# Norm boundaries: the last two squares summed on TensorE, products of high parts first, three first FFN tiles, and fillers in TensorE's pauses

## The chip, the cores and the metric

The kernel runs on one core of a Trainium2 chip. The metric is the device time of one execution in microseconds, taken as the median of several runs of the whole program. A profiled execution gives the trace that all rows below come from.

## What is computed

One step of a four-layer transformer backbone on 128 context tokens and 512 latent tokens (640 columns with margins: 644), model width 1024. Each layer is a token mixer followed by a gated ConvFFN, and each of the eight sub-layers starts with the same normalisation:

```python
def rmsnorm(x, g):
    y = x * rsqrt(mean(x * x, axis=-1) + EPS)
    return y * g
def modulate(h, shift, scale):
    return h * (1 + scale) + shift
...
for i in range(4):                     # mixers: pooling, GQA, differential, windowed GQA
    h = modulate(rmsnorm(x, norm1_g[i]), sh1, sc1)
    x = x + g1 * mixer_i(h)
    h = modulate(rmsnorm(x, norm2_g[i]), sh2, sc2)
    u = conv3(h @ w_in)                # 1024 -> 2 x 2816, three taps along the tokens
    a, b = split(u)
    x = x + g2 * ((silu(a) * b) @ w_out)
```

`sh`, `sc` and `g` come from a matrix product of the conditioning vectors with `w_mod` (1024 x 6144 for each layer). All arithmetic is float32.

## The kernel before

The state `x` lies transposed in SBUF as `xT`: eight slices (index d or k) of 128 channels by 644 columns. Every float32 product of the projections is made of three reduced-precision products: activations and weights are split into a high part (`h_hi`, `w_hi`) and a remainder (`h_lo`, `w_lo`), and `hi*hi`, `lo*hi` and `hi*lo` are summed in PSUM. `product` (L1941) issues these three for one output.

The order of the work is written out by hand, engine by engine; semaphores connect the engines. PSUM is two tensors of four banks: `psA` and `psB`.

**A norm boundary** is the place between the last product of one sub-layer and the first of the next. There are seven of them with the same code, n = 1 to 7 (the first norm of layer 0 has its own). Even n is the way from an FFN into the QKV products of layers 1, 2 and 3; odd n is the way from a mixer into the FFN. On the path lie:

- ScalarE squares each slice (`square`, L2165): slice 0 into `sq_sum`, slices 1 to 7 by turns into `sq[0]` and `sq[1]`.
- GpSimd adds slices 1 to 6 to `sq_sum` (`norm_pow`, L1892), VectorE adds slice 7 (L2337).
- TensorE sums over the 128 channels with the squares as stationary operand and a 128x2 tile of ones as the moving one (`norm_pe`, L1999; L2007), one product for each of five token tiles, into `psB`. The program's records show two matmuls for each, as for every plain float32 product here.
- VectorE turns the sums into means (`ms`, L2351), GpSimd takes the power -1/2 (`rs`, L1900), TensorE transposes and broadcasts it (L2017) to `psB`.
- VectorE scales each slice (`xs`, L2368), ScalarE adds the shift and rounds (`h_hi`, L2191), VectorE takes the remainder (`h_lo`, L2378). Two slices are in work at a time.

At n = 2 to 6 TensorE also runs a piece of the next modulation there (`mod_gap`, 64 short products of L1961 into `psA`, ahead of the sums, and its four transposes L1969 ahead of those of `rs`). At n = 1 it is `mod_raw(10)`, whose weights come by DMA.

**Even n, after the norm:** `qkv_step` (L2040). For each slice k, four output tiles (i = 0 to 3, token tiles, 512 columns each, one bank of `psA` each) get their three products; then i = 4 and on, tile by tile. ScalarE squares and copies tile i when its last product is done (L2225, L2226), VectorE and GpSimd norm and rotate it (L1463 and on), and VectorE's `w_lo` for the next weights (L2290) is queued behind the third of them.

**Odd n, after the norm:** `first_u_tiles` (L2090). Two FFN tiles (ft = 0, 1) of 128 channels by 644 columns (two halves of 322) are made together, slice by slice; then tile 2 and tile 3, each alone. ScalarE evacuates tile ft (`evac`, L2240), then makes two units of `w_hi` for the next weights (`split_next`), then evacuates tile ft + 1. Tile 2 uses the banks of tile 0, and tile 3 those of tile 1:

```python
def u_tile(it, ft, first):
    if not (first and ft < 2):
        pe.wait_ge(s_u[l], it * 4 + (ft - 1))
```

An FFN has 11 such rounds, and TensorE has no pause in one of them that matters here. `load_w`, `load_wo` and `load_m` are SyncE's DMA issues.

## Time and profile before

| | |
|---|---|
| median of 3 runs | 3270.67 us (3270.58 to 3274.07) |
| profiled execution, its own time | 3271.68 us |
| its span, first to last instruction | 3269.8 us |
| mean granted TensorE clock | 0.967 |
| TensorE matmul busy | 3083.9 us, 94% |
| VectorE, ScalarE, GpSimd busy | 2107.2, 1071.4, 403.9 us |
| the seven `ms` instructions (L2351) start at | 86.9, 617.0, 959.8, 1481.3, 1921.7, 2443.7 and 2776.7 us |

A row of the timeline gives start, duration, engine, line, operation and tiles; the bracket is the idle time of that engine before it and the instruction that ended it. Several instructions of one kind in a row are merged (x10). The granted clock is 1.00 at 2.4 GHz and 0.50 at 1.2 GHz.

### The profile page before, as it was taken

The page shows a single profiled execution, that of the slowest core. Times are in us where ns is not written, and L with a number is a line of the kernel's source. Part 1 is how long each engine was busy: PE and PEld are TensorE (multiplying, and loading weights), DVE is VectorE, ACT ScalarE, POOL GpSimd, SP SyncE. Part 2 cuts the span into 40 slices and gives each one's busy share as a digit, 9 for nine tenths or more (in the row PEclk, how much of TensorE's full clock was granted, in tenths as well). Part 3 has the DMA queues.
Part 4 walks back from the last instruction along what each step waited for, and adds up shares of the span by engine and source line. Part 5 has one row for each costly group of instructions (what it writes and reads, how often), then busy time and mean ns, then how long its engine had stood idle before and what let it go on. Part 6 is the DMA issues. An engine that isn't in the chain of part 4 may idle for free.

```text
span 3269.8 us, 54337 instructions
## 1 busy us (share of the span) xinstructions
PE 3083.9 (94%) x21098; PEld 2813.1 (86%) x21098; DVE 2107.2 (64%) x4290; ACT 1071.4 (33%) x2074; POOL 403.9 (12%) x392
## 2 busy tenths in 40 slices
PE   8999999888999999998989899999989888999998
PEld 6899999766599999997865699999987668999998
DVE  7666666567756666656646566666666674766665
ACT  3222222326623222223335432222223563322221
POOL 3000000123310000003237310000012231000000
PEclk9999999889999999999988999999999899999999
DMA  8533323110023332330200223333321002122211
GB/s 336 198 116 128 115 97 113 54 55 1 22 95 129 120 124 91 114 116 31 78 30 6 93 78 116 112 120 117 127 73 52 4 1 91 65 78 77 67 62 45
DMA packets 47188, 289.96 MB, mean 89 GB/s; under 512 B 4945, under 2 KB 11345, under 8 KB 13265
## 3 DMA queue, kind: packets, MB, share of 16 engines
q1 hardware_dynamic: 47058, 288.21, 24.2%
q8 instruction: 83, 1.36, 0.2%
q14 instruction: 47, 0.39, 0.0%
HBM read 283.98 MB, written 4.21 MB: 88 GB/s over the span
## 4 chain that ended last, share of the span: by engine, by line
PE 89%; DVE 6%; ACT 2%; issue 1%; DMA 1%; POOL 0%; SPq 0%; POOLq 0%; DVEq 0%; ACTq 0%
PE psA L1945 39%; PE psB L1945 25%; PE psA L2046 3%; PE psA L2048 3%; PE psA L2047 3%; PE psB L1961 2%; PE psA L779 2%; PE psB L712 2%; PE psB L694 1%; PE psB L837 1%; PE psA L680 1%; DVE top L1671 1%; DVE top L1558 1%; DVE query L1514 1%; DMA m_stage<-w_mod_dram 1%
## 5 line engine op out<-in xcount | busy, mean ns | idle before, releaser
L1945 PE MATMUL psA<-h_hi,w_hi 128*128 128x322 f32 (+1 forms) x2848 | 661.2, 314 | 13.7 <-DVE h_lo L2378 13.7
L1945 PE MATMUL psA<-h_lo,w_hi 128*128 128x322 f32 (+1 forms) x2832 | 657.7, 313 | 0.0
L1945 PE MATMUL psA<-h_hi,w_lo 128*128 128x322 f32 x2816 | 648.4, 311 | 0.0
L2405 DVE SCALAR_TENSOR_TENSOR xT<-psB,mod,xT 128x128 f32<-128x128 f32 x1128 | 425.4, 433 | 249.8 <-PE psB L1945 249.8
L1945 PEld LDWEIGHTS psA<-h_hi,w_hi 128*128 128x128 f32 x2848 | 481.3, 190 | 17.1 <-issue 15.7
L1945 PEld LDWEIGHTS psA<-h_lo,w_hi 128*128 128x128 f32 x2832 | 482.7, 190 | 0.0
L1945 PEld LDWEIGHTS psA<-h_hi,w_lo 128*128 128x128 f32 x2816 | 480.1, 190 | 0.0
L2459 DVE TENSOR_SCALAR conv<-u_raw,vec_sb 128x642 f32<-128x642 f32 x176 | 108.3, 615 | 468.6 <-ACT u_raw L2244 468.6
L2244 ACT ACTIVATE u_raw<-psA 128x644 f32<-128x644 f32 x176 | 124.6, 708 | 741.2 <-PE psA L1945 741.2
L2290 DVE TENSOR_TENSOR w_lo<-w_stage,w_hi 128x512 fp32r<-128x512 f32 x496 | 345.9, 743 | 27.1 <-ACT w_hi L2163 27.0
L1945 PE MATMUL psB<-g_hi,wo_hi 128*128 128x322 f32 x1408 | 335.6, 320 | 23.7 <-DVE g_lo L2480 23.7
L1945 PE MATMUL psB<-g_hi,wo_lo 128*128 128x322 f32 x1408 | 326.7, 314 | 0.0
L1945 PE MATMUL psB<-g_lo,wo_hi 128*128 128x322 f32 x1408 | 326.6, 313 | 0.0
L1898 POOL TENSOR_TENSOR sq_sum<-sq_sum,sq 128x644 f32<-128x644 f32 x42 | 71.3, 1698 | 1721.4 <-ACT sq L2180 1720.8
L1945 PEld LDWEIGHTS psB<-g_hi,wo_hi 128*128 128x128 f32 x1408 | 237.6, 192 | 38.2 <-DVE g_lo L2480 24.8
L2274 ACT ACTIVATE wo_hi<-wo_stage 128x1024 fp32r<-128x1024 f32 x88 | 88.4, 1053 | 554.5 <-PE psB L1945 554.5
L1945 PEld LDWEIGHTS psB<-g_lo,wo_hi 128*128 128x128 f32 x1408 | 241.2, 192 | 0.0
L1945 PEld LDWEIGHTS psB<-g_hi,wo_lo 128*128 128x128 f32 x1408 | 241.1, 191 | 0.0
L2046 PE MATMUL psA<-w_hi,h_lo 128*128 128x512 f32 x480 | 195.6, 408 | 26.0 <-DVE w_lo L2290 16.2
L2250 ACT ACTIVATE w_hi<-w_stage 128x512 fp32r<-128x512 f32 x344 | 196.7, 624 | 0.0
L2047 PE MATMUL psA<-w_hi,h_hi 128*128 128x512 f32 x480 | 193.4, 403 | 0.0
L2048 PE MATMUL psA<-w_lo,h_hi 128*128 128x512 f32 x480 | 193.2, 403 | 0.0
(257 smaller groups left out, 4526.3 us busy)
## 6 DMA issues: line engine op xcount, KB each, us to landing
w_stage<-weights_dram SPq DMA_DIRECT2D x124, 1024.0 KB, 4.9
m_stage<-w_mod_dram SPq DMA_DIRECT2D x96, 1024.0 KB, 8.3
wo_stage<-w_out_dram SPq DMA_DIRECT2D x44, 1024.0 KB, 4.8
yT_dram<-xT SPq DMA_DIRECT2D x8, 322.0 KB, 2.2
xT<-xT_dram SPq DMA_DIRECT2D x1, 1544.0 KB, 9.9
xT<-xT_dram SPq DMA_DIRECT2D x1, 1032.0 KB, 6.4
w_stage<-weights_dram SPq DMA_DIRECT2D x2, 512.0 KB, 17.8
rope_raw<-rope_dram SPq DMA_DIRECT2D x3, 256.0 KB, 2.7
```

The costliest lines, as they stand in the source:

```text
L712: ins = pe.matmul(OUT_LAT[odd * DH:(odd + 1) * DH, x:y], value(kt, 2 * d // GROUP), pt[(2 * d + odd) % 4][:, kt - 1, x:y], start=(kt == CA ...
L1898: pool.tensor_tensor(sq_sum[:, :], sq_sum[:, :], sq[d % 2][:, :], ALU.add).then_inc(s_sqsum, 1)
L1945: ins = pe.matmul(o, wp, xp[:, a:b], start=first and n == 0, stop=last and n == 2)
L2046: pe.matmul(o, hl, w_hi[:, k, :], start=(k == 0), stop=False)
L2047: pe.matmul(o, hh, w_hi[:, k, :], start=False, stop=False)
L2048: return pe.matmul(o, hh, w_lo[:, k, :], start=False, stop=(k == KT - 1))
L2244: act.activation(u_raw[ft % 2][:, :].rearrange("p (a n) -> p a n", a=2), psA[:, 2 * (ft % 2):2 * (ft % 2) + 2, 0:HALF], ACT.Copy).then_inc ...
L2250: act.activation(w_hi[:, u, :], w_stage[:, u, :], ACT.Copy).then_inc(s_whi, 1)
L2274: act.activation(wo_hi[:, f, :], wo_stage[:, f, :], ACT.Copy).then_inc(s_wohi, 1)
L2290: dve.tensor_tensor(w_lo[:, u, :], w_stage[:, u, :], w_hi[:, u, :].bitcast(F32), ALU.subtract).then_inc(s_wlo, 1)
L2405: ins = dve.scalar_tensor_tensor(out=xT[:, d, c:c + w], in0=psB[:, bank, at_:at_ + w], scalar=gate[:, d, i:i + 1], in1=xT[:, d, c:c + w], ...
L2459: own(dve.tensor_scalar(o[:, 1:1 + n], u[:, 1:1 + n], vcol(v + 1), vcol(v + 3), ALU.mult, ALU.add))
```

## The change

- **Sums.** VectorE's addition of slice 7 (L2337) goes, and GpSimd's of slice 6. TensorE now sums three tiles, `sq_sum` (slices 0 to 5), `sq[0]` (slice 6) and `sq[1]` (slice 7), each with five products, accumulated in `psA`, bank 0. Ahead of them one product with a tile of zeros (`zeros`, ten columns) clears the ten sums.
- **Fillers.** `keep_on(count, out)` runs `count` float32 products of the identity with a 128x128 tile of ones into a bank that nobody reads. Ten at n = 7 ahead of the sums; three ahead of the wait for `rs` (n = 2 to 7), six behind the transposes of `rs` (n = 2 to 7).
- **Order of products.** In the first group after each norm, the two products with `h_hi` of all tiles come first and wait for `h_hi` alone; those with `h_lo` follow. For i = 4 and on the order inside a step changes only.
- **Three tiles.** At n = 3, 5 and 7 tiles 0, 1 and 2 are made together; tile 2 goes to banks 0 and 1 of `psB`. At n = 1 it stays at two.

```diff
             def norm_pow(n):
                 m = n - 1
-                for d in range(1, KT - 1):
+                for d in range(1, KT - 2):
...
             def norm_pe(n, gap=None):
                 if gap is not None:
                     mod_gap(*gap)
+                elif n == 2 * DEPTH - 1:
+                    keep_on(10, psA[:, 0, :])
                 if n == 1:
                     pe.wait_ge(s_modok, MOD_PASSES - 2)
-                pe.wait_ge(s_sqall, n)
-                for j in range(NT):
-                    c = tile_col(j)
-                    ins = pe.matmul(psB[:, 0, 2 * j:2 * j + 2], sq_sum[:, c:c + P], ones2[:, :],
-                                    start=True, stop=True)
+                pe.matmul(psA[:, 0, 0:2 * NT], ident[:, :], zeros[:, :], start=True, stop=False, skip_group_check=True)
+                for i, x in enumerate((sq_sum, sq[0], sq[1])):
+                    if i == 0:
+                        pe.wait_ge(s_sqsum, (KT - 3) * n)
+                    pe.wait_ge(s_sq, KT * n - 2 + i)
+                    for j in range(NT):
+                        c = tile_col(j)
+                        ins = pe.matmul(psA[:, 0, 2 * j:2 * j + 2], x[:, c:c + P], ones2[:, :],
+                                        start=False, stop=(i == 2), skip_group_check=True)
                 ins.then_inc(s_stat, 1)
                 if gap is not None:
                     mod_gap_sum(*gap)
                 if n == 1:
                     mod_raw(10)
+                else:
+                    keep_on(3, psB[:, 1, :])
                 pe.wait_ge(s_rs, n)
...
                 ins.then_inc(s_bc, 1)
+                if n > 1:
+                    keep_on(6, psB[:, 1, :])
...
                     for k in range(KT):
                         pe.wait_ge(s_wlo, UNITS * c0 + k + 1)
+                        pe.wait_ge(s_hhi, KT * (2 * l - 1) + k + 1)
+                        for i in range(4):
+                            qkv_hi(i, k)
                         pe.wait_ge(s_h, KT * (2 * l - 1) + k + 1)
                         for i in range(4):
-                            ins = qkv_step(i, k)
+                            ins = qkv_lo(i, k)
                             if k == KT - 1:
                                 ins.then_inc(s_qp[l], 1)
...
+                    places = [halves(psA, 0), halves(psA, 1), halves(psB, 0)][:2 if l == 0 else 3]
...
-                dve.wait_ge(s_sqsum, (KT - 2) * n)
-                dve.wait_ge(s_sq, KT * n)
-                dve.tensor_tensor(sq_sum[:, :], sq_sum[:, :], sq[(KT - 1) % 2][:, :], ALU.add).then_inc(s_sqall, 1)
```

TensorE at the boundary n = 2, from the end of the modulation's products (L1961) to the first QKV products, before (`ones_139` is the 128x2 tile of ones):

```order
L1961 MATMUL psA<-m_stage_58,cond 32x128 x32
L2007 MATMUL psB<-ones_139,sq_sum 128x2 x5
L1969 MATMUL psA<-ident_sb,mod_rows 128x128 x4
L2017 MATMUL psB<-ident_sb,rs 128x128 x5
L2046 MATMUL psA<-w_hi,h_lo 128x512
L2047 MATMUL psA<-w_hi,h_hi 128x512
L2048 MATMUL psA<-w_lo,h_hi 128x512
```

and in the change:

```order
L1961 MATMUL psA<-m_stage_58,cond 32x128 x32
L2013 MATMUL psA<-zeros,ident_sb 128x10
L2020 MATMUL psA<-ones_139,sq_sum 128x2 x5
L2020 MATMUL psA<-ones_139,sq_67 128x2 x5
L2020 MATMUL psA<-ones_139,sq_68 128x2 x5
L1969 MATMUL psA<-ident_sb,mod_rows 128x128 x4
L2002 MATMUL psB<-ones,ident_sb 128x128 x3
L2032 MATMUL psB<-ident_sb,rs 128x128 x5
L2002 MATMUL psB<-ones,ident_sb 128x128 x6
L2063 MATMUL psA<-w_hi,h_hi 128x512
L2064 MATMUL psA<-w_lo,h_hi 128x512
```

Ten narrow products and one with the zeros came in ahead of the means, three fillers between the modulation's transposes and those of `rs`, and six ahead of the first product of the layer.

TensorE at n = 3, from the last transposes to the end of the first slice of the FFN's first tiles, in the change:

```order
L2032 MATMUL psB<-ident_sb,rs 128x128 x5
L2002 MATMUL psB<-ones,ident_sb 128x128 x6
L2133 MATMUL psA<-h_hi,w_hi 128x322 x2
L2133 MATMUL psA<-h_hi,w_lo 128x322 x2
L2133 MATMUL psA<-h_hi,w_hi 128x322 x2
L2133 MATMUL psA<-h_hi,w_lo 128x322 x2
L2133 MATMUL psB<-h_hi,w_hi 128x322 x2
L2133 MATMUL psB<-h_hi,w_lo 128x322 x2
L2138 MATMUL psA<-h_lo,w_hi 128x322 x4
L2138 MATMUL psB<-h_lo,w_hi 128x322 x2
```

Before, a slice was twelve products for two tiles, all behind `h_lo`; now it is eighteen for three, twelve of them ahead of `h_lo`, and the last products of tiles 0, 1 and 2 stand next to each other at the slice's end.

## Rows read from the trace of the kernel before

**Rows 1.** The page: the chain that ended last, share of the span by engine

```profile
PE 89%; DVE 6%; ACT 2%; issue 1%; DMA 1%; POOL 0%; SPq 0%; POOLq 0%; DVEq 0%; ACTq 0%
```

**Rows 2.** Timeline of the boundary n = 2 (start us, us, engine, line)

```profile
612.64 1.96 PE L1961 MATMUL psA<-m_stage,cond 128*32 128x128 f32 x64
...
614.76 0.83 DVE L2337 TENSOR_TENSOR sq_sum<-sq_sum,sq 128x644 f32<-128x644 f32 x1 [0.88 <-ACT sq L2180]
...
615.64 1.28 PE L2007 MATMUL psB<-ones,sq_sum 128*128 128x2 f32 x10 [1.05 <-DVE sq_sum L2337]
616.96 0.17 DVE L2351 TENSOR_SCALAR ms<-psB 128x5 f32<-128x5 f32 x1 [1.28 <-PE psB L2007]
...
618.44 1.33 PE L2017 MATMUL psB<-ident_sb,rs 128*128 128x128 f32 x5
...
623.05 0.77 PE L2046 MATMUL psA<-w_hi,h_lo 128*128 128x512 f32 x1 [3.29 <-DVE h_lo L2378]
```

**Rows 3.** Timeline of the boundary n = 3

```profile
954.53 1.38 ACT L2180 ACTIVATE sq<-xT 128x644 f32<-128x644 f32 x2
955.05 2.63 DVE L2290 TENSOR_TENSOR w_lo<-w_stage,w_hi 128x512 fp32r<-128x512 f32 x2
...
958.51 1.28 PE L2007 MATMUL psB<-ones,sq_sum 128*128 128x2 f32 x10 [2.67 <-DVE sq_sum L2337]
959.83 0.16 DVE L2351 TENSOR_SCALAR ms<-psB 128x5 f32<-128x5 f32 x1 [1.28 <-PE psB L2007]
...
963.97 1.93 ACT L2191 ACTIVATE h_hi<-xs,mod 128x128 fp32r<-128x128 f32 x4 [8.07 <-DVE xs L2368]
...
966.18 0.88 PE L1945 MATMUL psA<-h_hi,w_hi 128*128 128x322 f32 x2 [3.29 <-DVE h_lo L2378]
```

**Rows 4.** TensorE by stretches: length, busy (records), granted clock, DMA share, GB/s

```profile
623.00:628.30 5.30, 5.25 (x12) 0.50 0.00 0
956.00:959.50 3.50, 0.99 (x9) 1.00 0.26 47
966.10:969.60 3.50, 3.42 (x13) 0.50 0.00 0
970.00:973.00 3.00, 3.00 (x23) 1.00 0.00 0
...
93.00:99.40 6.40, 6.00 (x22) 0.50 1.00 419
```

**Rows 5.** Timeline of TensorE at n = 7

```profile
2774.33 2.30 PE L2007 MATMUL psB<-ones,sq_sum 128*128 128x2 f32 x10 [4.55 <-DVE sq_sum L2337]
...
2782.76 0.88 PE L1945 MATMUL psA<-h_hi,w_hi 128*128 128x322 f32 x2 [3.29 <-DVE h_lo L2378]
```

**Rows 6.** Timeline at the end of the first QKV group of layer 1

```profile
645.66 0.39 PE L2048 MATMUL psA<-w_lo,h_hi 128*128 128x512 f32 x1
...
646.09 0.60 ACT L2225 ACTIVATE qkv_sq<-psA 128x512 f32<-128x512 f32 x1 [11.26 <-PE psA L2048]
...
659.12 0.77 PE L2046 MATMUL psA<-w_hi,h_lo 128*128 128x512 f32 x1 [5.39 <-DVE w_lo L2290]
```

**Rows 7.** Timeline of ScalarE and TensorE after the FFN's first two tiles (n = 3)

```profile
981.52 0.71 ACT L2244 ACTIVATE u_raw<-psA 128x644 f32<-128x644 f32 x1 [3.55 <-PE psA L1945]
...
982.28 0.56 PE L1945 MATMUL psA<-h_hi,w_hi 128*128 128x322 f32 x2
...
983.17 0.70 ACT L2244 ACTIVATE u_raw<-psA 128x644 f32<-128x644 f32 x1
```

**Rows 8.** The chain in order of time: float32 products of 136 or 144 columns

```profile
20.90 2.10 PE psB L1064 x16
...
32.74 2.23 PE psA L1064 x8
```

**Rows 9.** Timeline of TensorE at n = 1

```profile
89.35 0.76 PE L2017 MATMUL psB<-ident_sb,rs 128*128 128x128 f32 x5
...
93.40 0.88 PE L1945 MATMUL psA<-h_hi,w_hi 128*128 128x322 f32 x2 [2.51 <-DVE h_lo L2378]
```

More of the change, by code:

```diff
@@ L232, in program @@
         ones = const("ones", [P, P])
+        zeros = const("zeros", [P, 2 * NT])
         sq_tok = const("sq_tok", [P, NT])
@@ L296, in program @@
         s_rs = sem("norm_rstd_ready")
-        s_sqall = sem("all_squares_added")
         s_bc = sem("rstd_broadcast")
@@ L1997, in mod_gap_sum, with keep_on @@
                 mod_sum(it * 2 + (MOD_PASSES * (2 * l + 1) + 2), [psA[:, c, 3 * P:] for c in range(4)])
+            def keep_on(count, out):
+                for _ in range(count):
+                    pe.matmul(out[:, 0:P], ident[:, :], ones[:, :], start=True, stop=True)
             def norm_pe(n, gap=None):
@@ L2040, in _, with qkv_hi, qkv_lo @@
                 else:
-                    def qkv_step(i, k):
+                    def qkv_hi(i, k):
                         o, col = psA[:, i % 4, :], tile_col(i % NT)
-                        hh, hl = h_hi[:, k, col:col + P], h_lo[:, k, col:col + P]
-                        pe.matmul(o, hl, w_hi[:, k, :], start=(k == 0), stop=False)
-                        pe.matmul(o, hh, w_hi[:, k, :], start=False, stop=False)
-                        return pe.matmul(o, hh, w_lo[:, k, :], start=False, stop=(k == KT - 1))
+                        hh = h_hi[:, k, col:col + P]
+                        pe.matmul(o, hh, w_hi[:, k, :], start=(k == 0), stop=False)
+                        pe.matmul(o, hh, w_lo[:, k, :], start=False, stop=False)
+                    def qkv_lo(i, k):
+                        o, col = psA[:, i % 4, :], tile_col(i % NT)
+                        return pe.matmul(o, h_lo[:, k, col:col + P], w_hi[:, k, :], start=False, stop=(k == KT - 1))
                     for k in range(KT):
                         pe.wait_ge(s_wlo, UNITS * c0 + k + 1)
+                        pe.wait_ge(s_hhi, KT * (2 * l - 1) + k + 1)
+                        for i in range(4):
+                            qkv_hi(i, k)
                         pe.wait_ge(s_h, KT * (2 * l - 1) + k + 1)
                         for i in range(4):
-                            ins = qkv_step(i, k)
+                            ins = qkv_lo(i, k)
                             if k == KT - 1:
@@ L2100, in first_u_tiles @@
                             mod_raw_sum(11)
+                        pe.wait_ge(s_hhi, KT * 2 * l + k + 1)
+                        for ft, outs in enumerate(places):
+                            u, c = 2 * ft + k // 4, (k % 4) * P
+                            for n, w in enumerate((w_hi, w_lo)):
+                                for o, (a, b) in outs:
+                                    pe.matmul(o, w[:, u, c:c + P], h_hi[:, k, a:b], start=(k == 0 and n == 0), stop=False)
                         pe.wait_ge(s_h, KT * 2 * l + k + 1)
-                        for ft in range(2):
+                        for ft, outs in enumerate(places):
                             u, c = 2 * ft + k // 4, (k % 4) * P
-                            ins = product(halves(psA, ft), (w_hi[:, u, c:c + P], w_lo[:, u, c:c + P]),
-                                          (h_hi[:, k, :], h_lo[:, k, :]), k == 0, k == KT - 1)
-                            if ft == 0 and k in (3, 7):
-                                ins.then_inc(s_wused, 1)
-                    ins.then_inc(s_wused, 2)
+                            for o, (a, b) in outs:
+                                ins = pe.matmul(o, w_hi[:, u, c:c + P], h_lo[:, k, a:b], start=False, stop=(k == KT - 1))
+                            if k == 3 and ft == 0 or k == 7:
+                                ins.then_inc(s_wused, 2 if ft else 1)
                 def out_pass(it, last=False):
@@ L2138, in ffn_iter @@
                         mod_ffn(l, 0, 1)
-                    u_tile(it, 2, first)
+                    if not first or l == 0:
+                        u_tile(it, 2, first)
                     if not first and l < DEPTH - 1:
@@ L2243, in evac @@
                         act.wait_ge(s_conv[l], it * 4 + (ft - 1))
-                    act.activation(u_raw[ft % 2][:, :].rearrange("p (a n) -> p a n", a=2),
-                                   psA[:, 2 * (ft % 2):2 * (ft % 2) + 2, 0:HALF], ACT.Copy).then_inc(s_u[l], 1)
+                    src = psB[:, 0:2, :] if first and l and ft == 2 else psA[:, 2 * (ft % 2):2 * (ft % 2) + 2, :]
+                    act.activation(u_raw[ft % 2][:, :].rearrange("p (a n) -> p a n", a=2), src[:, :, 0:HALF],
+                                   ACT.Copy).then_inc(s_u[l], 1)
                 def split_next(it, ft):
@@ L2413, in _ @@
             own(dve.memset(ones2[:, :], 1.0))
+            own(dve.memset(zeros[:, :], 0.0))
             own(dve.memset(ones[:, :], 1.0))
```

11 lines of the change are left out of this document (6 added, 5 removed).

## The prediction, as put on record before the changed kernel was run

> **What bounds the kernel now.** I read the chain that ended last first: TensorE holds 89% of it, VectorE 6% [rows 1]. So time is won where TensorE pauses or runs at half clock, and lost where it gets more to do or waits longer. Then the timeline of the boundaries, for who ends each pause. At n = 2 TensorE is done with the modulation at 614.60 (612.64 + 1.96), VectorE's addition starts at 614.76, the ten narrow records take 1.28 us, the means come at 616.96, and the first QKV product starts at 623.05 [rows 2]. At n = 3 the squares are there at 955.91, but VectorE is busy with two `w_lo` for 2.63 us, and TensorE sums only at 958.51; means at 959.83, first product at 966.18, while the first slice of `h_hi` is done half of 1.93 us after 963.97, at 964.94 [rows 3]. Last the granted clock by stretches: it is 1.00 while TensorE does little but the narrow products (0.99 us busy in 3.5), then 0.50 into the first products: 5.3 us of products at n = 2 and 3.5 at n = 3 [rows 4].
>
> **The sum, forecast case: the clock falls as before.** All lengths are against before; M is the start of the means.
>
> 1. *Sums.* 30 narrow records and 2 for the zeros replace 10. At 1.28/10, less the tail of the last, one costs 0.12 us [rows 2], so 32 take 3.9. At even n they run from 614.60, to 618.5, and M is 1.6 us later: before, TensorE had only waited 1.05 us there. At n = 3 and 5 they run from 955.85 to 959.75 against M at 959.83: nothing. VectorE's addition, its `w_lo` slowed by GpSimd (1.3 us each) and the wait for them were in the way before; TensorE's own work takes exactly their place. At n = 7 there is no modulation; ten fillers (term 2) last 2.6 us, then 3.9, from about 2769.8: M at 2776.3 against 2774.33 + 2.30 = 2776.63: -0.3. At half clock a narrow record costs 0.23 [rows 5]; the fall can come in the midst of them. Bounds 0 and +1.5 us at each place, taken as +0.4, since most positions of the fall lie near their end.
> 2. *Three fillers.* One is two records. Float32 products of 136 to 144 columns go at 0.131 us a record at full clock and 0.279 at half [rows 8]; I take 0.13 and, for 128 columns, 0.26. Three cost 0.8 or 1.6 us. At n = 2 to 6 they stand between the modulation's transposes, which wait for two copies by VectorE, and those of `rs`. The latter started 1.48 us after M at n = 2 [rows 2], with `rs` just ready, so there is no pause to fill: the cost is whole, 0.75 at full clock, 1.6 at half. At n = 7 the wait for `rs` (1.4 us) covers them: 0.
> 3. *High parts first.* The first product waits for `h_hi` and no longer for `h_lo`: 966.18 - 964.98 = 1.2 us earlier [rows 3]. But six fillers stand ahead of it, 1.6 us at full clock and 3.1 at half, beside 2.05 us for the first `xs` and `h_hi`. At half clock they end last by 0.95; the fillers are long enough that the clock may be back before they end, so I take 0.3. Net -0.9, at n = 7 -0.2 (nothing else delays the fillers there).
> 4. *Cold products.* TensorE now works without a pause from M + 0.9 to its first product, longer than the 3.5 to 5.3 us of products after which the clock came back before [rows 4], so the first products run at full clock. Saved: half of the cold stretch. At 0.233 against 0.426 us a QKV product, 5.3 us lose 2.4 [rows 4]; n = 4 and 6, read the same way, lost 2.0 and 2.1. At 0.149 against 0.267 an FFN product, 3.5 us lose 1.56 [rows 4]; n = 5 lost 1.9 and n = 7 1.35.
> 5. *QKV group, even n.* A chain of ScalarE, VectorE and GpSimd starts when tile i = 0 has its last product, 646.09, and releases TensorE 13 us later, after a pause of 5.39 us [rows 6]. In the last slice tile 0's third product had nine behind it; now it has three. With 0.233 us each, the chain starts 1.4 us later against the group's end, and nothing covers it. +1.4.
> 6. *Three tiles, n = 3, 5, 7.* Tile 3 needs the banks of tile 1. ScalarE evacuates tile 0, makes two `w_hi`, evacuates tile 1: from 981.52 to 983.17 + 0.70, 2.35 us. Tile 2 covered that; TensorE went on at 982.28 [rows 7]. Now tile 0's last product is five records before the group's end, and TensorE waits for both: 2.35 less about 0.4: +1.9. What three tiles give is that TensorE cannot run dry for `h`: a slice is 2.7 us of products, against 1.96 us for VectorE's work on it. Before it was 1.8, but started late and cold and never ran dry, so there is nothing to win unless the clock holds.
>
> Even n: 1.6 + 0.4 + 1.6 - 0.9 - 2.2 + 1.4 = +1.9, with the cold transposes of n = 2 (full clock before) +2.1; three of them 6. n = 3 and 5: 0.4 + 1.6 - 0.9 - 1.7 + 1.9 = +1.3 each, 2.6. n = 7: 0.1 - 0.2 - 1.35 + 1.9 = +0.4. n = 1: 22 records more, 2.6 us, ahead of `mod_raw(10)` and the transposes, less 1.2 for `h_hi`; before, TensorE was idle 2.51 us ahead of 93.40 [rows 9] and then half as fast for 6.4 us [rows 4], and a later start may keep the clock. Bounds -1.8 and +1.1: I take 0. Removing GpSimd's addition and VectorE's costs and gives nothing more. Sum **+9 us** on the profiled execution's 3271.68, or 3280.7; the median lies 1.0 under that execution: **3280**.
>
> **Why the clock should fall.** Between the modulation's products and its transposes TensorE now has only products of two columns for nearly 4 us, and then the copies' pause of 0.9. In the trace of before ten of them, and what little stood beside them, never held it: 956.0 to 959.5 is such a stretch, and half clock follows [rows 4]. The fillers stand behind, not in it; the ten at n = 7 stand ahead. The Trainium skill, "TensorE: Matmul & The Clock Gate", section "Why this matters for your kernels", asks only that there be no long gaps in which TensorE idles between bursts. By that rule the narrow products would keep it and the first rival holds; the rows lean the other way.
>
> **Rival 1, the clock holds (0.25): faster.** Its place is the stretch of sums, and it decides at the point where narrow products count as work. Then term 1's 0.4 goes, term 2 is 0.75, the transposes of `rs` take 0.76 us as at n = 1 [rows 9] and not 1.3 (-0.55), the six fillers are covered, and the cold products are saved whole. Even n: 1.6 + 0.75 - 0.55 - 1.2 - 2.2 + 1.4 = -0.2 to -0.3; n = 3 and 5: 0.75 - 0.55 - 1.2 - 1.75 + 1.9 = about -1; n = 7: -1.5; n = 1: -1.8. Sum -6.6: 3264, between 3261 and 3269. For it: the fillers are there in all the other pauses. Against it: rows 4.
>
> **Rival 2, the fillers do not bring it back (0.1): slower still.** Then the change does not do what it says: term 4 returns (11 us in all) and six fillers at half clock cost 0.65 more at five places. 3280 + 11 + 3 = 3294. The same skill page, section "Part 4: PE-mode transpose", says that transposes don't count as work for the clock; at full weight that speaks for this rival. But the fillers are plain products, and dense ones brought it back at every boundary before.
>
> **Rival 3, a cover (0.1): no change.** Term 5 or 6 is partly hidden by a wait that is there anyway, say VectorE's or GpSimd's; 1 us less at each of six places gives 3274. Against it: rows 6 and 7 show the wait ended by just those chains.
>
> **The numbers.** Forecast 0.55, its own range 3275 to 3287; rival 1 0.25, rival 2 0.1, rival 3 0.1. The range that leaves out no more than 2 in 10 reaches into rival 1 and short of rival 2: 3262 to 3289. 0.2% is 6.5 us (about what can be told from no change): faster, under 3264.1, is half of rival 1 and its odd neighbours, 0.2; same, to 3277.2, is the rest of it, rival 3 and the forecast's lower end, 0.3; slower 0.5.
>
> **What would show it.** Right: half clock from within or just behind the thirty narrow records; means 1.6 us or more later after the modulation at even n and level at n = 3; the transposes of `rs` starting 2.2 us (full clock) or 3.4 (half) after M; first products at full clock; the pause of 5.4 us in QKV unchanged or longer, and counted from tile 0; a new pause of about 2 us of TensorE before tile 3, ended by ScalarE's `u_raw`, at three places. Wrong: a clock of 1.00 through a whole boundary, narrow records faster than 0.12 us, or no pause before tile 3.

## The result, and the profile after

The changed kernel takes 3285.87 us (median of 6, 3275.59 to 3289.9) against 3274.1 us for the kernel before (median of 6, 3270.58 to 3277.71): 1.003 of its time, 95% interval 1.0018 to 1.0042, so slower by 11.8 us. The profiled execution of the changed kernel is the fastest of its six. A second series of both, among the experiments, gave 3283.7 against 3271.3 us, a ratio of 1.0037 (1.0024 to 1.0051); the profile taken there (run e1_same, span 3283.8 us, itself 3285.54 us) is of an ordinary execution, so rows of both are read.

Page of the changed kernel, the lines that answer to [rows 1] and to the table of before:

```profile
span 3273.8 us, 54877 instructions
...
PE 89%; DVE 6%; ACT 2%; issue 1%; DMA 1%; POOL 0%; SPq 0%; POOLq 0%; DVEq 0%; ACTq 0%
...
L1945 PE MATMUL psA<-h_hi,w_hi 128*128 128x322 f32 (+1 forms) x2672 | 617.6, 312 | 5.5 <-ACT u_raw L2278 5.5
```

TensorE keeps its 89% of the chain. In the page of before the row of these products has 13.7 us of pauses, ended by `h_lo`; new are 5.5 us of pauses ended by ScalarE's `u_raw`, which are the three pauses ahead of tile 3.

Timeline of the changed kernel at n = 2, against [rows 2] (L2020 sums, L2002 fillers, L2032 transposes of `rs`, L2063 first QKV product):

```profile
610.66 1.95 PE L1961 MATMUL psA<-m_stage,cond 128*32 128x128 f32 x64
...
612.79 1.26 PE L2020 MATMUL psA<-ones,sq_sum 128*128 128x2 f32 x10
613.91 2.37 PE L2020 MATMUL psA<-ones,sq 128*128 128x2 f32 x20
616.32 0.17 DVE L2381 TENSOR_SCALAR ms<-psA 128x5 f32<-128x5 f32 x1 [4.33 <-PE psA L2020]
...
619.39 0.97 PE L2032 MATMUL psB<-ident_sb,rs 128*128 128x128 f32 x5
620.20 1.50 PE L2002 MATMUL psB<-ones,ident_sb 128*128 128x128 f32 x12
...
622.60 0.47 PE L2063 MATMUL psA<-w_hi,h_hi 128*128 128x512 f32 x1 [0.90 <-ACT h_hi L2224]
```

From the start of the modulation's products to the means it was 4.32 us and is 5.66: 1.34 later, since the thirty records stand one behind the other and nothing fills in for them. From the means to the transposes of `rs` it was 1.48 and is 3.07: the three fillers. The first product comes 6.28 us behind the means where it came 6.09 behind; the wait is ended by `h_hi` now. And it starts at full clock. TensorE by stretches, the first three answering to the first three in [rows 4], the last one behind tile 3's start (stretch, length, busy with records, granted clock, DMA share, GB/s):

```profile
622.60:626.00 3.40, 3.40 (x15) 1.00 0.00 0
956.00:959.50 3.50, 2.57 (x19) 0.76 0.68 267
966.00:969.50 3.50, 3.50 (x26) 1.00 0.00 0
988.70:991.90 3.20, 3.20 (x13) 0.50 0.00 0
```

So in this profile the clock fell within or behind the sums at every boundary and was back by the first products or within the first few, as forecast. The last row was not forecast. Ahead of it stands the pause before tile 3, here in the timeline of n = 3, against [rows 7]:

```profile
985.58 0.71 ACT L2278 ACTIVATE u_raw<-psA 128x644 f32<-128x644 f32 x1 [8.44 <-PE psA L2138]
...
986.18 1.14 ACT L2284 ACTIVATE w_hi<-w_stage 128x512 fp32r<-128x512 f32 x2
...
987.22 0.70 ACT L2278 ACTIVATE u_raw<-psA 128x644 f32<-128x644 f32 x1
...
987.97 0.56 PE L1945 MATMUL psA<-h_hi,w_hi 128*128 128x322 f32 x2 [1.84 <-ACT u_raw L2278]
```

ScalarE's two evacuations with two `w_hi` between them are bare now: 1.84 us of pause, and then 3.2 us of products at 1.2 GHz. And this is the end of the first QKV group of layer 1, against [rows 6]:

```profile
644.46 0.60 ACT L2258 ACTIVATE qkv_sq<-psA 128x512 f32<-128x512 f32 x1 [9.03 <-PE psA L2069]
...
645.60 0.49 PE L2063 MATMUL psA<-w_hi,h_hi 128*128 128x512 f32 x1 [0.47 <-ACT qkv L2259]
...
657.49 0.77 PE L2063 MATMUL psA<-w_hi,h_hi 128*128 128x512 f32 x1 [6.06 <-DVE w_lo L2324]
```

The pauses there add up to 6.53 us where there was one of 5.39, and the same two stand at the other two even boundaries.

The split sums cost most at n = 1. Timeline of the changed kernel, and then the same rows of e1_same:

```profile
84.58 1.26 PE L2020 MATMUL psA<-ones,sq_sum 128*128 128x2 f32 x10
85.70 2.82 PE L2020 MATMUL psA<-ones,sq 128*128 128x2 f32 x20
...
88.56 0.16 DVE L2381 TENSOR_SCALAR ms<-psA 128x5 f32<-128x5 f32 x1 [4.07 <-PE psA L2020]
```

```profile
84.69 2.27 PE L2020 MATMUL psA<-ones,sq_sum 128*128 128x2 f32 x10
86.83 4.41 PE L2020 MATMUL psA<-ones,sq 128*128 128x2 f32 x20
...
91.27 0.16 DVE L2381 TENSOR_SCALAR ms<-psA 128x5 f32<-128x5 f32 x1 [6.87 <-PE psA L2020]
```

And the kernel before:

```profile
86.89 0.16 DVE L2351 TENSOR_SCALAR ms<-psB 128x5 f32<-128x5 f32 x1 [1.16 <-PE psB L2007]
```

The squares are long there, but the sums stand behind TensorE's wait for the modulation. So all thirty are on the path, and the means wait 4.07 us for them where the clock falls only near their end and 6.87 where it has fallen ahead of them, in place of 1.16.

### The profile page after: what moved, and what is told of

Same layout as the page of the kernel before. It is cut to its first block, busy times and chain, and to the rows that moved or that the text cites. A ratio compares the mean times of both kernels' runs of the same rounds, so it can differ in the third digit from the quotient of the medians.

```text
span 3273.8 us, 54877 instructions
## 1 busy us (share of the span) xinstructions
PE 3112.8 (95%) x21380; PEld 2843.2 (87%) x21380; DVE 2097.1 (64%) x4284; ACT 1071.3 (33%) x2074; POOL 392.1 (12%) x385
## 4 chain that ended last, share of the span: by engine, by line
PE 89%; DVE 6%; ACT 2%; issue 1%; DMA 1%; POOL 0%; SPq 0%; POOLq 0%; DVEq 0%; ACTq 0%
PE psA L1945 36%; PE psB L1945 25%; PE psA L2063 3%; PE psA L2064 3%; PE psA L2069 3%; PE psB L1961 2%; PE psA L779 2%; PE psB L712 2%; PE psA L2133 1%; PE psB L694 1%; PE psB L837 1%; PE psA L680 1%; PE psA L2020 1%; DVE top L1671 1%; PE psA L2138 1%
## 5 line engine op out<-in xcount | busy, mean ns | idle before, releaser
L1945 PE MATMUL psA<-h_hi,w_hi 128*128 128x322 f32 (+1 forms) x2672 | 617.6, 312 | 5.5 <-ACT u_raw L2278 5.5
L1945 PE MATMUL psA<-h_lo,w_hi 128*128 128x322 f32 (+1 forms) x2656 | 615.0, 312 | 0.0
L1945 PE MATMUL psA<-h_hi,w_lo 128*128 128x322 f32 x2640 | 606.8, 311 | 0.0
L1945 PEld LDWEIGHTS psA<-h_hi,w_hi 128*128 128x128 f32 x2672 | 450.1, 190 | 6.9 <-ACT u_raw L2278 6.3
L1945 PEld LDWEIGHTS psA<-h_lo,w_hi 128*128 128x128 f32 x2656 | 450.9, 189 | 0.0
L1945 PEld LDWEIGHTS psA<-h_hi,w_lo 128*128 128x128 f32 x2640 | 448.6, 190 | 0.0
L1898 POOL TENSOR_TENSOR sq_sum<-sq_sum,sq 128x644 f32<-128x644 f32 x35 | 59.5, 1699 | 1704.7 <-ACT sq L2213 1704.3
L2063 PE MATMUL psA<-w_hi,h_hi 128*128 128x512 f32 x480 | 192.5, 401 | 21.3 <-DVE w_lo L2324 18.2
L2069 PE MATMUL psA<-w_hi,h_lo 128*128 128x512 f32 x480 | 179.0, 397 | 0.0
```

The lines of the kernel that those rows point to most:

```text
L1945: ins = pe.matmul(o, wp, xp[:, a:b], start=first and n == 0, stop=last and n == 2)
L2063: pe.matmul(o, hh, w_hi[:, k, :], start=(k == 0), stop=False)
L2069: return pe.matmul(o, h_lo[:, k, col:col + P], w_hi[:, k, :], start=False, stop=(k == KT - 1))
```

## The experiments

Each was timed in 5 rounds beside the kernel before on the same chip; the medians of before in the four series, on three chips, are 3271.3, 3271.0, 3271.18 and 3270.63 us.

**How to tell the boundaries from the rest.** Two executions of one kernel can lie several us apart, and not at the boundaries: inside the attention of layers 1 to 3 TensorE falls to half clock in other places from profile to profile. So I divide each profiled execution at marks that every version has:

- *to n = 2*: from the start to the modulation's products at n = 2, with the boundary n = 1 in it;
- *sums*: at n = 2 to 6 from the modulation's first product to the means, at n = 7 from the end of the last product of the mixer to the means, six in all;
- *behind, even*: from the means of n = 2, 4 and 6 to TensorE's first product behind the pause for `w_lo` [rows 6];
- *behind, odd*: from the means of n = 3, 5 and 7 to the start of ScalarE's sixth `u_raw`;
- *attention*: what lies between the marks of an even boundary and the next odd one.

The rest, the FFNs of layers 1 to 3, is 1374.0 to 1375.9 us in all of them. Lengths in us, worked out from the timelines; each is of one execution:

| profiled execution | to n = 2 | sums | behind, even | behind, odd | attention |
|---|---|---|---|---|---|
| before | 612.6 | 31.7 | 126.0 | 153.8 | 971.4 |
| the change | 610.7 | 35.1 | 124.3 | 157.2 | 971.8 |
| e1_same | 611.4 | 35.9 | 124.5 | 156.5 | 981.0 |
| e2_two_tiles | 609.9 | 36.5 | 124.4 | 152.0 | 973.9 |
| e3_qkv_last_slice | 611.0 | 35.1 | 120.1 | 155.0 | 978.3 |
| e4_no_fillers | 613.1 | 32.3 | 127.2 | 161.8 | 972.3 |
| e5_both_repairs | 612.2 | 34.6 | 120.3 | 152.8 | 975.4 |
| e6_old_sums | 607.4 | 30.7 | 119.9 | 152.7 | 972.7 |
| e7_wide_sums | 615.2 | 36.2 | 115.5 | 149.1 | 971.8 |
| e8_hi_first_alone | 607.9 | 31.7 | 123.8 | 154.0 | 975.6 |
| e9_old_sums_wide | 604.9 | 31.0 | 118.6 | 152.8 | 973.0 |
| e10_no_fillers | 607.1 | 32.1 | 123.3 | 153.9 | 976.0 |
| e11_old_sums_n1 | 608.0 | 35.2 | 120.5 | 152.6 | 977.1 |
| e12_rstd_first | 606.3 | 30.7 | 120.1 | 152.6 | 973.2 |

The attention column spreads over 9.6 us, more than most of the effects below. That it goes with the clock shows in its longest piece, layer 2 from n = 4 to n = 5. Two stretches there, both from 14 us behind the means of n = 4 to 7 us ahead of those of n = 5, first in e9_old_sums_wide and then in e10_no_fillers:

```profile
1485.80:1902.32 416.52, 381.33 (x1828) 0.94 0.14 51
```

```profile
1488.26:1911.20 422.94, 388.36 (x1834) 0.92 0.14 50
```

Why a version shows one pattern or the other, no run tells.

**The change again.** No edit.

> The changed kernel once more, beside the three that follow. Theory A (the clock falls in the narrow sums, the fillers bring it back, and the three costs of the prediction stand): 0.2 to 0.4% above the kernel before, 3278 to 3288 us, half clock again behind the sums at each of the seven boundaries. Theory B (the loss is the place at which the clock happens to fall and differs from execution to execution): in this profile at least two boundaries keep full clock, and the median lies within 0.1% of the kernel before.

Measured: 3283.7 us (3282.93 to 3287.52), 1.0037 (1.0024 to 1.0051) of before. This is what the next three are held against. Half clock stands at all seven boundaries, so theory B fails in its own terms. For the size it has a point: against the profile of before, e1_same is 14.0 us longer, and 9.6 of these lie in the attention, where the clock falls in other places.

**Two first tiles.**

```
-                    places = [halves(psA, 0), halves(psA, 1), halves(psB, 0)][:2 if l == 0 else 3]
+                    places = [halves(psA, 0), halves(psA, 1), halves(psB, 0)][:2]
...
-                    if not first or l == 0:
-                        u_tile(it, 2, first)
+                    u_tile(it, 2, first)
```

> The FFN starts with two tiles at n = 3, 5 and 7, as before; all else as changed. Theory A: the pause of TensorE before tile 3 (about 2 us at three places) goes; TensorE may run dry for h now and then, up to 0.2 us a slice, so 3 to 5.5 us less than the changed kernel. Theory C (three tiles pay, because TensorE would starve with two at full clock): as slow or slower than the changed kernel, with pauses of TensorE that end with h_hi or h_lo of more than 2 us at each place.

Measured: 3274.9 us (3271.77 to 3280.39), 1.0011 (1.0001 to 1.002), 8.8 us below e1_same, more than either theory allowed. Page of this run, the row for ScalarE's pauses; then TensorE behind tile 3's start at n = 3, in e1_same:

```profile
L1945 PE MATMUL psA<-h_hi,w_hi 128*128 128x322 f32 (+1 forms) x2720 | 627.6, 312 | 1.5 <-ACT u_raw L2277 1.5
```

```profile
988.00:990.00 2.00, 0.56 (x4) 1.00 0.00 0
990.00:991.50 1.50, 1.10 (x7) 1.00 0.00 0
991.50:995.00 3.50, 3.50 (x15) 0.51 0.00 0
```

The pauses fall from 5.5 to 1.5 us. With the pause the fall of the clock behind it goes too: it stands in e1_same behind two of the three places (here, and behind tile 3 of the last FFN), in this run behind none. A fall of about 3.4 us at 1.2 GHz loses 1.7 us, so 4.0 + 3.4 = 7.4 us come back there. But something is paid for it: with two tiles at full clock TensorE does run dry for `h_lo`, as theory A allowed. Its products with `h_lo`, slice by slice at n = 3, start every 1.96 us, which is VectorE's pace, where twelve records take 1.8:

```profile
969.81 0.87 PE L2138 MATMUL psA<-h_lo,w_hi 128*128 128x322 f32 x4
...
971.77 0.88 PE L2138 MATMUL psA<-h_lo,w_hi 128*128 128x322 f32 x4
```

Net, the odd boundaries are 4.5 us shorter (156.5 to 152.0). The rest of the 8.8 us lies elsewhere: the attention is 7.1 us shorter in this profile.

**The last slice of the QKV group tile by tile.**

```
-                        for i in range(4):
-                            qkv_hi(i, k)
+                        if k < KT - 1:
+                            for i in range(4):
+                                qkv_hi(i, k)
                         pe.wait_ge(s_h, KT * (2 * l - 1) + k + 1)
                         for i in range(4):
+                            if k == KT - 1:
+                                qkv_hi(i, k)
                             ins = qkv_lo(i, k)
```

> In the first QKV group the last slice (k = 7) goes tile by tile again, the other seven with high parts first. Theory A: the chain that starts with tile 0's last product starts 1.4 us earlier at n = 2, 4 and 6: 4 us less than the changed kernel. Rival: VectorE or GpSimd is late there anyway, under 1 us.

Measured: 3275.59 us (3269.36 to 3278.66), 1.0008 (0.9999 to 1.0017), 8.1 us below e1_same. The wait is back at the 5.39 us of before:

```profile
656.55 0.77 PE L2063 MATMUL psA<-w_hi,h_hi 128*128 128x512 f32 x1 [5.39 <-DVE w_lo L2327]
```

It is so at all three even boundaries. By the waits that is 1.14 us at each; from the means to the end of the pause it is 1.57, 1.37 and 1.44, together 4.4 us (124.5 to 120.1), as theory A has it. The other 3.7 us are not the edit's as far as the traces show: 2.7 us of attention, and a fall of the clock behind one tile 3 less.

**Without fillers.** All calls of `keep_on` are out.

> No fillers at all. Theory A: three fillers ahead of the transposes cost 0.8 to 1.3 us at five places, but the clock comes back later, with 2 us lost at six places: 0 to 8 us more than the changed kernel. Rival (fillers only delay, the clock does not follow them): 4 to 8 us less than the changed kernel.

Measured: 3282.74 us (3279.46 to 3284.27), 1.0032 (1.002 to 1.0043): 1 us below e1_same, within what the two medians can tell. In its trace the clock stays down into the first products at n = 3 (0.88 us for the first pair, where it was 0.53), while the first product comes 5.29 us behind the means and not 6.30. The traces say why the median hardly moves. Behind the means this run is 8.0 us longer than e1_same (2.7 at even n, 5.2 at odd n), the sums are 3.6 shorter, half of that the ten fillers of n = 7, and the attention happens to be 8.7 shorter. So the fillers pay at the boundaries here as well, and the attention hides it.

**Both repairs together.** The edits of e2_two_tiles and of e3_qkv_last_slice.

> The change with both repairs together: only two first FFN tiles, and the last slice of the QKV chain tile by tile. Theory A (each of the two gives back its own wait and the half-clock stretch behind it, apart from the other): the 8.8 us of e2_two_tiles and the 8.1 us of e3_qkv_last_slice add up, 3283.7 - 16.9 = 3267, below the kernel before. Theory B (the waits proper are 5.5 us before tile 3 plus about 1.7 us of half clock behind each of one to three of them, and 1.1 us x 3 in the QKV group, and the rest of both results was which stretches of the attention fell to the half clock in those executions): 3283.7 - 9 to -12 = 3272 to 3275.

Measured: 3273.69 us (3271.96 to 3274.82), 1.0005 (0.9996 to 1.0014). Theory B: 10.0 us below e1_same, where the two single results add up to 16.9 and the waits and falls seen in the traces to 10.8. So what the single runs gave beyond that was not theirs. Behind the means the trace has 7.9 us for both (4.2 at even n, 3.7 at odd n), and the pauses are those of the single runs.

**The sums of before.** On e5_both_repairs.

```
-                for d in range(1, KT - 2):
+                for d in range(1, KT - 1):
...
+                dve.wait_ge(s_sqsum, (KT - 2) * n)
+                dve.wait_ge(s_sq, KT * n)
+                dve.tensor_tensor(sq_sum[:, :], sq_sum[:, :], sq[(KT - 1) % 2][:, :], ALU.add).then_inc(s_sqall, 1)
...
-                pe.matmul(psA[:, 0, 0:2 * NT], ident[:, :], zeros[:, :], start=True, stop=False, skip_group_check=True)
-                for i, x in enumerate((sq_sum, sq[0], sq[1])):
...
+                pe.wait_ge(s_sqall, n)
+                for j in range(NT):
+                    c = tile_col(j)
+                    ins = pe.matmul(psB[:, 0, 2 * j:2 * j + 2], sq_sum[:, c:c + P], ones2[:, :],
+                                    start=True, stop=True)
```

> e5_both_repairs with the sums of the kernel before: POOL adds squares 1 to 6, VectorE adds the last, and TensorE makes one set of five products. Theory A (the prediction's term for the split sums: 16 us x 0.1, that is 1.6 us later means at each of the three even boundaries, and an earlier fall of the clock at all of them): 4 to 8 us below e5. Rival (the split sums take as much out of the odd boundaries, or keep the engine busy where it would idle, as they cost at the even ones): within 2 us of e5, or above it.

Measured: 3260.2 us (3259.5 to 3262.12), 0.9964 (0.9951 to 0.9977): 13.5 us below e5_both_repairs and 10.8 below the kernel before. That is 5.5 more than I expected at most, so the split sums are the dearest part of the change. Its timeline at n = 2:

```profile
607.42 1.95 PE L1962 MATMUL psA<-m_stage,cond 128*32 128x128 f32 x64
...
610.42 1.28 PE L2017 MATMUL psB<-ones,sq_sum 128*128 128x2 f32 x10 [1.05 <-DVE sq_sum L2369]
...
614.75 1.27 PE L2029 MATMUL psB<-ident_sb,rs 128*128 128x128 f32 x5
...
618.26 0.47 PE L2060 MATMUL psA<-w_hi,h_hi 128*128 128x512 f32 x1 [0.78 <-ACT h_hi L2223]
```

The means are back at 4.32 us behind the modulation (611.74), and with the fillers the clock is back before the first product, which takes 0.47 us (0.77 at half clock, in [rows 2]).

**Wide sums.** On e5_both_repairs, with `ones[:, 0:64]` as the moving operand in place of the two columns of `ones2`, the sums 64 columns apart, and `zeros` as wide. TensorE's records are no longer for it: at full clock ten take 1.22 us where they took 1.26.

> e5_both_repairs with 64 columns in place of 2 in each product of the sums (the same sums in every column). Theory A (the half clock comes because products of two columns keep TensorE busy in the records but do not count for the clock): the fall in the sums goes or moves behind the wait for rs, less half clock at each boundary, and 3 to 10 us below e5. Rival (the waits around the sums drop the clock whatever the sums hold): the same places of the falls, within 2 us of e5.

Measured: 3267.21 us (3256.3 to 3268.88), 0.9982 (0.9973 to 0.9991), 6.5 us below e5_both_repairs. This is the stretch from 5 us ahead of the means to 13 us behind them, at n = 1, 2 and 3, in e5_both_repairs and then with wide sums:

```profile
85.85:103.85 18.00, 16.20 (x109) 0.74 0.73 309
613.11:631.11 18.00, 17.06 (x127) 0.81 0.09 30
953.52:971.52 18.00, 17.07 (x149) 0.81 0.18 59
```

```profile
87.83:105.83 18.00, 16.20 (x95) 0.64 0.64 266
616.17:634.17 18.00, 16.17 (x130) 1.00 0.10 30
956.23:974.23 18.00, 16.18 (x147) 1.00 0.18 59
```

At all six boundaries from n = 2 on the clock is 1.00 throughout, with the same waits, the same number of records issued and the same fillers. So from n = 2 on it was the narrow operand that let the clock fall. Behind the means that gives 8.6 us (120.3 to 115.5 and 152.8 to 149.1); the means themselves come up to 0.37 us later, since the product with `zeros` is 320 columns wide now. At n = 1 the clock fell before the sums began, and they cost more than ever. The Trainium skill, "TensorE: Matmul & The Clock Gate", section "Why this matters for your kernels", asks only for no long gaps between bursts; here the records alone, without a gap, did not hold the clock, so on this point the trace disagrees.

**High parts first, alone.** On the kernel before, the split into `qkv_hi` and `qkv_lo` and the same order for the two first FFN tiles, the last QKV slice tile by tile.

> The kernel before with one part of the change alone, the high parts ahead of the low parts (the last slice of the QKV chain tile by tile). By the prediction's term of 0.9 us at six boundaries: 5 us below the kernel before, 3266. Rival (the first products run at the half clock there, so that the start moves ahead but the chain is set by TensorE behind it, or the clock's return takes what was won): within 2 us of the kernel before.

Measured: 3269.36 us (3268.23 to 3271.7), 0.9992 (0.9983 to 1.0001): 1.6 us below before, its interval reaches 1. The first product does come 5.31 us behind the means at n = 2 in place of 6.09, and the wait is ended by `h_hi`, but it starts cold:

```profile
617.52 0.77 PE L2046 MATMUL psA<-w_hi,h_hi 128*128 128x512 f32 x1 [2.24 <-ACT h_hi L2207]
...
607.21:625.21 18.00, 13.78 (x113) 0.72 0.10 31
```

So the median says the rival. The trace says where it holds: at n = 3, 5 and 7 nothing is left at the sixth `u_raw` (154.0 against 153.8; e2_two_tiles shows VectorE's pace for `h` setting the length there); at the even boundaries 2.3 us are won, and 4.7 by n = 2, at n = 1, where the stretch at half clock is half as long as before. The attention was 4.1 us longer in this profile.

**The sums of before, wide.** On e6_old_sums, 64 columns in its five products.

> e6_old_sums with 64 columns in place of 2 in its five products a boundary. In e7 thirty wide ones held the clock at every boundary; in e6 ten records of two columns are still followed by 3.4 us at half clock at each of six boundaries. Theory A (columns, not records, hold the clock, and ten wide records do it as well): these six stretches go, 1.7 us each in the work done, up to 10 us: 3250 to 3256. Rival (with so few records it is the pause before and behind them that drops it): as e6, 3260, within 2 us.

Measured: 3261.84 us (3256.68 to 3267.39), 0.9973 (0.9964 to 0.9982). The rival: no gain over e6_old_sums (the medians differ by 1.6 us the other way). In the stretches around the means the clock is 1.00 at n = 1 and 2, 0.91 at n = 3 to 6 and 0.81 at n = 7. At n = 3 VectorE's addition leaves a pause of 2.67 us ahead of the sums, but at n = 4 and 6 the pause is that of n = 2 (1.0 us) and the clock falls all the same. So ten wide products did not hold it as thirty did; which of the pauses around them decides is not shown.

**The same without fillers.** On e9_old_sums_wide, no `keep_on`.

> e9_old_sums_wide without any of the fillers. Theory A (the change's fillers bring the clock back in the waits for rs and h_hi, which is what pays; in e4 they paid nothing because the thirty narrow records had used the place up): 5 to 10 us above e9. Rival (with wide sums there is enough dense work at a boundary without them, and they stand in the way of rs's transposes): within 2 us of e9 or below it.

Measured: 3268.11 us (3266.91 to 3271.41), 0.999 (0.9981 to 0.9999), 6.3 us above e9_old_sums_wide. The stretches around the means at n = 3 and 7, first of e9_old_sums_wide, then of this run:

```profile
944.89:962.89 18.00, 13.50 (x115) 0.91 0.18 59
...
2757.36:2775.36 18.00, 14.89 (x91) 0.81 0.18 58
```

```profile
947.71:965.71 18.00, 12.17 (x92) 0.72 0.18 58
...
2768.14:2786.14 18.00, 11.69 (x57) 0.62 0.17 58
```

0.72 and 0.62 are also what the kernel before has at these two places. So the fillers do what the change says. What they pay can be read behind the means: 4.7 us at the even boundaries and 1.0 at the odd ones, and 1.0 more in the sums of n = 7, 6.8 in all and near the difference of the medians. The two profiled executions lie 10.3 apart; the rest is mostly attention (3.1) and the stretch to n = 2 (2.1), which holds no filler. At n = 3 the fillers win nothing: the sixth `u_raw` starts 51.43 us behind the means with them and 51.45 without.

**The sums of before at n = 1 alone.** On e5_both_repairs.

```
+                if n == 1:
+                    pe.wait_ge(s_sqall, 1)
+                    for j in range(NT):
+                        c = tile_col(j)
+                        ins = pe.matmul(psB[:, 0, 2 * j:2 * j + 2], sq_sum[:, c:c + P], ones2[:, :],
+                                        start=True, stop=True)
+                else:
```

> e5_both_repairs with the sums of the kernel before at n = 1 alone (POOL adds six squares there, VectorE the last, one set of five products); the split sums stay at the other six boundaries. In the traces the thirty records stand there wholly in the path, behind the wait for the modulation: 4.1 us from the first to the means in the profiled run of the change and 6.9 in that of e1_same, where the kernel before has 1.3. Theory A (this is a term of its own, which the prediction set at nothing): 3 to 5 us below e5, 3269 to 3271, and the remaining 9 us to e6 are the even boundaries and the falls within the sums. Rival (DMA ends the start of the first FFN there, so a later norm is hidden): within 1 us of e5.

Measured: 3269.93 us (3268.31 to 3271.07), 0.9995 (0.9986 to 1.0003), 3.8 us below e5_both_repairs: theory A. The means of n = 1 come at 87.40 in place of 90.85, 3.45 sooner, which bears it out. The remaining 9.7 us to e6_old_sums I had put down to the other boundaries. Their stretches at n = 2 and 3, in this run and then in e6_old_sums:

```profile
609.85:627.85 18.00, 16.17 (x91) 0.81 0.07 24
950.94:968.94 18.00, 16.23 (x149) 0.91 0.18 59
```

```profile
606.74:624.74 18.00, 15.24 (x135) 0.91 0.10 31
948.34:966.34 18.00, 13.50 (x119) 0.91 0.18 59
```

At the even boundaries the mean granted clock over the 18 us is 0.10 lower with the split sums. That is no price of its own on top of the later means: where the clock falls inside the sums, the means are later for it (6.88 us behind the modulation's first product at n = 2, 5.66 and 5.65 at n = 4 and 6, where e6_old_sums has 4.32, 4.31 and 4.32), and behind the means the two differ by 0.4 us in all. At n = 3 the clock is equal, and the means come no later. So the traces show 5.2 us of later means at the even boundaries, less 0.7 of earlier ones at the odd ones, plus 0.4: some 5.0 of the 9.7. Another 4.4 us is attention.

**`rs` ahead of the modulation at n = 1.** On e6_old_sums: TensorE transposes `rs` between the two halves of `mod_raw(10)`, and VectorE's `mod_raw_copy(10)` stands behind `scaled(0)`.

> e6_old_sums, the fastest version so far, with the modulation moved out of the way at n = 1: TensorE transposes rs between the two halves of the modulation's products (the second waits for its DMA until 87.38 in e6's trace, while rs is there at 87.0), and VectorE copies the modulation's sums behind the first xs and no longer ahead of the transposed rs. By e6's rows xs starts at 90.61 and the first FFN product at 92.81; with the transposes at 87.1 xs starts at 87.9, the copy follows at 88.9, the modulation's transposes at 89.7, and the first product at 90.4. Theory A (nothing behind n = 1 waits for DMA in that stretch): 2.4 us below e6, 3257.8. Rival (the products then run into the wait for the DMA of the next modulation or of weights): e6's 3260, within 1 us.

Measured: 3259.75 us (3258.96 to 3264.1), 0.9968 (0.9956 to 0.998). The medians say the rival, 0.45 us. The first FFN product does come sooner, 4.49 us behind the means of n = 1 in place of 7.24, and from these means to those of n = 2 it is 523.75 us (86.84 to 610.59) against 526.17 (85.57 to 611.74) in e6_old_sums. But that is no proof of the edit: e9_old_sums_wide, without it, has 523.77 (85.55 to 609.32), with a first product 5.61 us behind the means. What this run and that one share is a clock of 1.00 behind the means of n = 1, where e6_old_sums has 3.4 us at half clock. So nothing shows a gain from the edit itself.

## Why the prediction was right, and where it was not

The forecast case came about: the clock falls in or behind the sums, the fillers bring it back, and the kernel is slower. The time lay 5.9 us above the forecast, of which about 3 are the series itself, since before measured 3274.1 in it and 3270.67 when I wrote. Against before I had said +9; it was +11.8 and +12.4.

That the size fits so well is in good part luck. Divided at the marks of the table, my sum and the two profiles of the change, all against before:

| | forecast | the change | e1_same |
|---|---|---|---|
| n = 1 (to n = 2) | 0 | -2.0 | -1.2 |
| sums | +6.9 | +3.4 | +4.2 |
| behind, even | -0.1 | -1.8 | -1.5 |
| behind, odd | +2.2 | +3.3 | +2.7 |
| attention | 0 | +0.3 | +9.6 |
| sum, with the rest of the FFNs | +9.0 | +4.0 | +14.0 |

The boundaries proper cost about 3 to 4 us and not 9. What lifts the ordinary execution over the forecast is half clock in the attention, for which I had no term. So the direction and the mechanism at the boundaries are borne out, and the size is reached by another way. Term by term:

1. *Sums.* The means came 1.34 us later at n = 2 where I had 1.6, 0.28 earlier at n = 3 where I had 0, and at n = 7, counted from the end of the last product, 5.90 us behind it where it was 6.87. Right in kind. Of the term for the falls, 0.4 at each boundary, the odd ones show nothing, and at the even ones it shows where the clock falls inside the sums: 1.03 us at n = 6 of the change, 0.74 and 1.14 at n = 2 and 4 of e1_same. At **n = 1** the split sums alone cost much: the means' wait grew by 2.9 us in one execution and by 5.7 in the other, and e11_old_sums_n1 has 3.8 us for it in the time. I had 2.6 for the records and set them off against an earlier `h_hi` and a clock kept by a later start. Half of that failed and half held: the records cost more than 2.6, and by n = 2 it was regained, so that against before the place is 1.2 to 2.0 us shorter, within or just outside my bounds. (The upper bound, +1.1, does not come out of its own terms, 2.6 - 1.2 = 1.4.)
2. *Three fillers.* Their price was right: 1.6 us from the means to the transposes of `rs` at half clock, as written. From n = 3 on, where these transposes started 1.8 us behind the means before, it is 1.3.
3. *High parts first.* 0.8 us at n = 2 and 1.0 at n = 3 alone, in place of 1.2. With the fillers in the way the change has nothing of it at n = 2: 6.28 against 6.09 us.
4. *Cold products saved.* Right at the even boundaries: 0.233 us a QKV product from the first on; e10_no_fillers shows 6.3 us for the fillers after their own cost, and 4.7 of it there in the trace. At the odd ones it holds with three tiles (5.2 us longer without fillers, e4_no_fillers) and hardly with two (1.0, e10_no_fillers), where VectorE's 1.96 us for each slice of `h` sets the pace once the products are fast.
5. *QKV group.* 1.46 us each by e3_qkv_last_slice, where I had 1.4: one loop order gives it back, and the pause of 5.39 with it.
6. *Three tiles.* A pause of 1.84 us where I had 1.9, ended by `u_raw`. I left out two things. A new pause also costs clock: half clock behind two of the three in both profiles of the change, 1.7 us each. And I said that there was nothing to win unless the clock holds; the fillers do bring it back before the first products, and then two tiles run dry for `h`. Net, three tiles cost 1.9, 0.7 and 1.9 us in the traces, least where the clock did not fall.

Rival 1 was refuted for two columns. For 64 columns its clock came about: with e7_wide_sums it stays at 1.00 over six boundaries. That is the cleanest confirmation of the reason I gave against it. (Its parts as listed add up to -6.1 and not -6.6; that changes nothing.) Rivals 2 and 3 did not come about.

What the parts are worth, read down the chain of runs: three tiles and the QKV order together 10.0 us (3283.7 to 3273.69), the split sums 3.8 at n = 1 and 9.7 at the others (to 3269.93 and to 3260.2). The traces find 7.9 of the 10.0, the 3.8, and 5.0 of the 9.7 at the boundaries, and the rest mostly in the attention. On the other side stand the fillers, 6.3 us by the medians and 6.8 by the marks, and the high parts first, 1.6 by the medians and 7 by the marks, of which 4.1 were lost in that execution's attention. So the change holds two parts that pay (fillers, high parts first) and three that cost (the split sums, three first tiles, the order of the last QKV slice); with only the paying ones the kernel takes 3260.2 us, 0.9964 of before.

One thing stays open. Between the fastest execution of the change and the median lie 10 us, and the two profiles place them in the start (2.7 us by the means of n = 1) and in the attention: from the means of n = 6 to those of n = 7 it is 331.97 us in one and 336.35 in the other, from n = 4 to n = 5 439.75 and 443.41. TensorE falls to half clock there in other places in each. Whether the change's shift of the program makes the slower pattern more likely was not settled, and with one profile for each version the marks cannot tell what is an edit's doing there and what is chance.

## What to carry to other kernels

Work moved onto the engine that bounds the kernel is free only where that engine would have stood still for as long as it takes, at each place where it occurs: follow the same edit through every boundary in the trace, the odd one out (here n = 1, where a wait for something else held the sums back) first. Before a difference of medians is given to an edit, divide the traces at marks around the place that it changes: here up to 9.6 us lay in attention, far from the boundaries. A faster clock pays only where TensorE sets the pace: ask which engine is next. Every new pause of TensorE is to be costed twice, once as time and once as the products at 1.2 GHz behind it. And where a release at the end of a group starts a chain on other engines, keep the order that finishes the first tile early, even if the rest of the group runs in another.

## What the runs showed of the hardware

- A product of two columns and one of 64 cost TensorE the same time (ten records 1.26 and 1.22 us), but thirty of the first came with half clock, in them or behind them, at every boundary (e5_both_repairs) and thirty of the second at none from n = 2 on (e7_wide_sums). Widening the moving operand cost the sums nothing there (the means came up to 0.37 us later for the wider product with `zeros`) and kept 2.4 GHz. Ten wide ones kept it at n = 2 and not at n = 3 to 7.
- Plain products on constant data brought the clock back in pauses: the granted clock over the 18 us around n = 3 was 0.91 with them (e9_old_sums_wide) and 0.72 without (e10_no_fillers).
- A pause of 1.84 us between dense products was followed by half clock in some places and not in others of the same execution.
- VectorE's two `w_lo` at n = 3 took 2.63 us while GpSimd added, [rows 3], and 1.28 us in the changed kernel, where GpSimd was idle:

```profile
953.21 1.28 DVE L2324 TENSOR_TENSOR w_lo<-w_stage,w_hi 128x512 fp32r<-128x512 f32 x2
```
